# A state-space recurrence taken over pairs of tokens, inside a fused transformer layer

## What is computed

```python
a_bar = jnp.exp(lam * dt)                      # complex, 32 groups x 64 states
b_coef = (a_bar - 1.0) / lam
bu = lax.complex(bu_re, bu_im) * b_coef        # bu_re = einsum('blgi,gni->blgn', u, b_re)
_, state = lax.associative_scan(combine, (a_seq, bu), axis=1)   # s[t] = a_bar s[t-1] + bu[t]
y = einsum(real(state), c_re) - einsum(imag(state), c_im) + d_skip * uf
y = jax.nn.gelu(y); out = y * jax.nn.sigmoid(y @ w_glu + b_glu)
```

## Time and profile before

| | us |
|---|---|
| median of 3 runs | 2065.24 |
| lowest, highest | 2062.25, 2070.86 |
| the profiled execution | 2072.4 |
| its span, first to last instruction | 2070.5 |
| mean granted TensorE clock in it | 0.963 |

### The profile page before, as it was taken

One profiled execution on the slowest core, in us unless ns is written; L12 is line 12 of the kernel. 1 busy time (PEld: TensorE's weight loads), 2 busy tenths in 40 slices (PEclk: granted clock), 3 DMA queues, 4 the chain that ended last, 5 costly groups with the idle time before them and its releaser, 6 DMA issues.

```text
span 2070.5 us, 21878 instructions
## 1 busy us (share of the span) xinstructions
PE 1975.8 (95%) x8614; PEld 1516.5 (73%) x8614; DVE 1247.4 (60%) x1646; ACT 846.2 (41%) x1269; POOL 387.3 (19%) x343
## 2 busy tenths in 40 slices
PE   7999999989977899999999999999999899999997
PEld 5888888766532478888888777776788778766786
DVE  6764344597796445655664776925773468536742
ACT  5331333201445633322333446645552357455531
POOL 2000000156244010100001202512400013214102
PEclk9999999998778899999999989999999999999998
DMA  4232232221000124554552222222122222220221
GB/s 185 85 126 82 95 107 97 85 64 71 26 0 1 66 79 164 196 202 148 198 200 75 82 91 80 82 82 82 52 91 92 97 83 82 91 83 31 92 92 61
DMA packets 53317, 196.69 MB, mean 95 GB/s; under 512 B 5984, under 2 KB 6496, under 8 KB 52704
## 3 DMA queue, kind: packets, MB, share of 16 engines
q1 hardware_dynamic: 43200, 160.55, 22.3%
q0 software_dynamic: 7504, 28.58, 4.1%
q10 hardware_dynamic: 2512, 6.18, 0.9%
HBM read 192.14 MB, written 2.10 MB: 94 GB/s over the span
## 4 chain that ended last, share of the span: by engine, by line
PE 77%; DVE 16%; ACT 4%; issue 2%; POOL 1%; DMA 1%; SPq 0%; POOLq 0%; DVEq 0%; ACTq 0%
PE PS L571 76%; DVE AR L1590 3%; DVE WLO L1587 3%; DVE AR L1823 2%; DVE AR L2072 1%; ACT WHI L1116 1%; PE PS L790 1%; DVE TMP L2146 1%; DVE AR L1913 1%; DVE AR L2039 0%; DVE HNL L1590 0%; DVE ACC L1590 0%; DMA RAW<-in_w13a 0%; DVE H L1975 0%; POOL ACC L2322 0%
## 5 line engine op out<-in xcount | busy, mean ns | idle before, releaser
L1587 DVE TENSOR_TENSOR WLO<-RAW,WHI 128x1024 fp32r<-128x1024 f32 (+1 forms) x272 | 378.3, 1394 | 509.2 <-ACT WHI L1116 509.2
L571 PE MATMUL PS<-HNH,WHI 128*128 128x512 f32 x1632 | 657.9, 403 | 16.0 <-ACT HNH L1147 14.1
L571 PE MATMUL PS<-HNH,WLO 128*128 128x512 f32 x1632 | 640.6, 393 | 3.8 <-DVE WLO L1587 3.8
L1116 ACT ACTIVATE WHI<-RAW 128x1024 fp32r<-128x1024 f32 (+1 forms) x272 | 297.6, 1095 | 648.0 <-PE PS L571 577.1
L571 PE MATMUL PS<-HNL,WHI 128*128 128x512 f32 x1632 | 436.7, 390 | 0.4
L571 PEld LDWEIGHTS PS<-HNH,WHI 128*128 128x128 f32 x1632 | 308.6, 189 | 96.9 <-issue 22.3
L571 PEld LDWEIGHTS PS<-HNH,WLO 128*128 128x128 f32 x1632 | 308.8, 189 | 78.7 <-issue 9.3
L571 PEld LDWEIGHTS PS<-HNL,WHI 128*128 128x128 f32 x1632 | 307.3, 188 | 66.4 <-DVE HNL L1590 2.6
L2202 POOL TENSOR_TENSOR ACC<-ACC,SQ 128x512 f32<-128x512 f32 x46 | 62.9, 1367 | 786.4 <-ACT SQ L1131 785.4
L571 PE MATMUL PS<-AR 128*128 128x512 f32 (+12 forms) x652 | 181.9, 515 | 6.5 <-DVE SQ L1807 5.8
L571 PEld LDWEIGHTS PS<-AR 128*128 128x128 f32 (+5 forms) x652 | 86.3, 203 | 76.8 <-issue 53.0
(11 more groups left out here) (314 smaller groups left out, 2475.6 us busy)
## 6 DMA issues: line engine op xcount, KB each, us to landing
RAW<-in_w_in SPq DMA_DIRECT2D x80, 512.0 KB, 3.5
AR<-in_w_ada POOLq DMA_DIRECT2D x48, 512.0 KB, 3.8
RAW<-in_w13a SPq DMA_DIRECT2D x44, 512.0 KB, 3.2
RAW<-in_w13b SPq DMA_DIRECT2D x44, 512.0 KB, 4.2
RAW<-in_w_out SPq DMA_DIRECT2D x40, 512.0 KB, 3.5
RAW<-in_w2a SPq DMA_DIRECT2D x16, 704.0 KB, 4.1
RAW<-in_w2b SPq DMA_DIRECT2D x16, 704.0 KB, 5.5
RAW<-in_w_inA SPq DMA_DIRECT2D x12, 512.0 KB, 3.3
```

The costliest lines, as they stand in the source:

```text
L571: return pe.matmul(o, l, r, start=start, stop=stop, skip_group_check=True)
L1116: act.activation(hi_of(name, i), raw_of(name, i), ACT.Copy).then_inc(*HI.up(name, i))
L1587: dve.tensor_tensor(lo_of(name, i), raw_of(name, i), f32(hi_of(name, i)), S_).then_inc(*LO.up(name, i))
```

## The change

State is kept at odd tokens only. U is stored with its even tokens first and its odd tokens behind them, 256 each. For a pair (2k, 2k+1) the drive is B u[2k+1] + (a_bar B) u[2k]: two sets of input weights, SA for even and SB for odd tokens, accumulated in PSUM, real and imaginary part side by side in one bank. The scan then runs over 256 pairs with |a_bar| squared, in two chunks of 128; the tables are those of the doubled angle. The output at odd tokens is C' times the state as before. At even tokens it is (C' a_bar) times the state of the pair before, plus a direct product of u[2k] with the 32x32 blocks of C'B (THRU), since the pair's own even state isn't kept. The weights SA, Ca and THRU are computed on the chip: 12 operations of 128x512 more on DVE (three each for CaR, CaI, ATr and ATi), and copies of the results out of PSUM, 8 transposes and 32 products of 32x32 outputs on PE after step 6 of half 0. The schedule of the parameter pieces becomes: two pieces in steps 0 to 3, one in 7 and 8, two in 9 to 12. The output of the mixer is put back in token order when it is split into halves. To make room, OL, U, V_, XAp and the temporaries move; the load of c waits for the last product of w_out.

```diff
 def s5_order():
     for b in range(-1, 9):
         if 0 <= b < 8:
-            for c in range(4):
+            for c in range(2):
                 yield "scan", b, c
...
+            def s5_weights():
+                for z, src in enumerate((ATr, ATi)):
+                    ps, b = take(pe, "s5_a", z)
+                    pe.wait_ge(*V.at("s5_at"))
+                    for y4 in range(4):
+                        t = pe.transpose(ps[:, P * y4:P * y4 + P], src[:, 4 * y4:4 * y4 + 4, :].rearrange("p a b -> p (a b)"), IDENT)
...
+                ps, b = take(pe, "s5_thru")
+                for t16 in range(16):
+                    y4, r = t16 // 4, 32 * (t16 % 4)
+                    o = ps[r:r + 32, P * y4 + r:P * y4 + r + 32]
+                    mm(o, BTr[:, t16, :], CpR[:, t16, :], True, False)
+                    t = mm(o, BTi[:, t16, :], CpI[:, t16, :], False, True)
...
+                        if z == "a" and (half, mi) == (0, 6):
+                            s5_weights()
...
                 elif step == "drive":
                     b, j = at_
-                    mm(psR[:, :], SBr[r, y4, :], U[r, y4, :], True, True).then_inc(*P_.up("drive_re", t16))
-                    psI, bI = take(pe, "drive_im", t16)
-                    mm(psI[:, :], SBi[r, y4, :], U[r, y4, :], True, True).then_inc(*P_.up("drive_im", t16))
...
+                    if j == 0:
+                        bs = [take(pe, "drive", 2 * b + x) for x in range(2)]
+                        for half, (even, odd) in enumerate(((SAr, SBr), (SAi, SBi))):
+                            for e, w in enumerate((even, odd)):
+                                for x, (ps, _) in enumerate(bs):
+                                    r = slice(32 * (2 * (b % 2) + x), 32 * (2 * (b % 2) + x) + 32)
+                                    ts[x] = mm(ps[:, HT * half:HT * half + HT], w[r, y4, :], U[r, y4, HT * e:HT * e + HT], e == 0, e == 1)
...
                 elif step == "read":
+                    mm(ps[r, 0:HT], THRU[r, y4, r], U[r, y4, 0:HT], True, False)
                     for z in range(4):
-                        for j in range(2):
+                        for now in (True, False):
+                            for j in range(2):
...
+                                if now:
+                                    t = mm(o[:, HT:T], w[:, t16, :], x, False, z == 3)
+                                else:
+                                    t = mm(o[:, 1:HT], w[:, t16, :], x[:, 0:HT - 1], False, z == 3)
...
+                tt(RHO, RHO, RHO, M_)
...
+                for o, (x1, y1), (x2, y2), op in ((CaR, (CpR, ar_), (CpI, ai_), A_), (CaI, (CpI, ar_), (CpR, ai_), S_),
+                                                  (ATr, (BTr, ar_), (BTi, ai_), S_), (ATi, (BTi, ar_), (BTr, ai_), A_)):
+                    tt(w1, x1, y1, M_)
+                    tt(w2, x2, y2, M_)
+                    tt(o, w1, w2, op, "s5_at")
+                    if o is CaI:
+                        yield
...
-                    if half == 0 and i < 10:
+                    if half == 0 and (i < 4 or i in (7, 8) or 9 <= i < 13):
                         next(params, None)
-                        next(params, None)
+                        if i not in (7, 8):
+                            next(params, None)
...
                 elif step == "drive":
-                    dve.tensor_tensor(f4(vr), f4(psR[:, :]), c4, M_).then_inc(*V.up("drive_a", t16))
-                    dve.tensor_tensor(f4(t1), f4(psI[:, :]), s4, M_).then_inc(*V.up("drive_b", t16))
-                    dve.tensor_tensor(f4(vi), f4(psI[:, :]), c4, M_).then_inc(*V.up("drive_im", t16))
-                    dve.tensor_tensor(f4(t2), f4(psR[:, :]), s4, M_).then_inc(*V.up("drive", t16))
+                    dve.tensor_tensor(f4(V_[b % 2][:, j, :]), f4(ps[:, :]), c4, M_).then_inc(*V.up("drive_a", t16))
+                    if b:
+                        dve.wait_ge(*G.at("drive_im", t16 - 2))
+                    dve.tensor_tensor(f4(S5T[j]), f4(ps[:, :]), s4, M_).then_inc(*V.up("drive", t16))
...
-                    stt(f4(S5T[k2]), f4(V_[b % 2][1][:, j, :]), -1.0, tables(t16)[1], M_, M_).then_inc(*V.up("back_im", t16))
+                    stt(f2(S5T[j][:, HT:T]), f2(V_[b % 2][:, j, HT:T]), -1.0, tables(t16, 2)[1], M_, M_).then_inc(*V.up("back_im", t16))
...
-            pool.dma_start(AR[:, 4096:6144], D["s5_bc"]).then_inc(*loaded("s5_bc").up())
+            pool.dma_start(AR[:, 4096:5120], D["s5_bc"][:, 0:1024]).then_inc(*loaded("s5_bc").up())
+            pool.dma_start(AR[:, 0:2048], D["s5_bc"][:, 1024:3072]).then_inc(*loaded("s5_bc").up())
+            pool.memset(RR, 0.0).then_inc(*G.up("s5_zero"))
...
                 elif step == "drive":
-                    pool.tensor_tensor(vr, vr, S5T[k1], A_).then_inc(*G.up("drive_re", t16))
-                    pool.tensor_tensor(vi, vi, S5T[k2], S_).then_inc(*G.up("drive_im", t16))
+                    pool.tensor_tensor(vr, vr, S5T[j][:, HT:T], A_).then_inc(*G.up("drive_re", t16))
+                    pool.tensor_tensor(vi, vi, S5T[j][:, 0:HT], S_).then_inc(*G.up("drive_im", t16))
...
-                    pool.tensor_tensor(f4(S5T[2 * j]), f4(vr), s4, M_).then_inc(*G.up("back_re", t16))
-                    pool.tensor_tensor(f4(vr), f4(vr), c4, M_).then_inc(*G.up("back_vr", t16))
-                    pool.tensor_tensor(f4(vi), f4(vi), c4, M_).then_inc(*G.up("back_vi", t16))
+                    pool.tensor_tensor(f2(S5T[j][:, 0:HT]), f2(v[:, 0:HT]), s2, M_).then_inc(*G.up("back_re", t16))
+                    pool.tensor_tensor(f4(v), f4(v), c4, M_).then_inc(*G.up("back_v", t16))
...
+            pool.wait_ge(*P_.at("w_out", KD - 1))
             pool.dma_start(CB, D["c"].partition_broadcast(P)).then_inc(*loaded("c").up())
```

More of the change, by code:

```diff
@@ L468, in sm @@
             return SMALL[:, 16 * i:16 * i + 16]
-        V_ = [[ar(at_v, 2, T) for at_v in pair] for pair in ((9216, 10240), (11264, 12288))]
-        XAp = ar(5120, 2, T)
+        V_ = [ar(10240 + 1024 * i, 2, T) for i in range(2)]
+        XAp = ar(12288, 2, T)
         XBp = ar(19456, 16, 2, 31)
-        CEf = ar(5120, 1024)
+        CEf = ar(12288, 1024)
         CE = CEf.rearrange("p (a b c) -> p a b c", b=8, c=32)
@@ L1614, in s5_params @@
             def s5_params():
-                dt, x, th, k, r, cs, sn, t1, t2, arr, aii, br, bi, den = (sm(i) for i in range(14))
+                dt, x, th, k, r, cs, sn, t1, t2, arr, aii, br, bi, den, are, aim = (sm(i) for i in range(16))
                 lr, li = vec("a_re"), vec("a_im")
@@ L1676, in s5_params @@
                 yield
+                ar_, ai_ = bc(are, 2, b3), bc(aim, 2, b3)
+                for o, (x1, y1), (x2, y2), op in ((CaR, (CpR, ar_), (CpI, ai_), A_), (CaI, (CpI, ar_), (CpR, ai_), S_),
[5 more added lines that the diff above has]
+                        yield
+                tt(t1, cs, cs, M_)
+                tt(t2, sn, sn, M_)
+                tt(sn, cs, sn, M_)
+                tt(cs, t1, t2, S_)
+                ts(sn, sn, 2.0, None, M_)
+                yield
+                for z, o in enumerate((SAr, SAi)):
+                    dve.wait_ge(*P_.at("s5_a", z))
+                    dve.tensor_copy(o, bank("s5_a", z)[:, :].rearrange("p (y n) -> p y n", n=P)).then_inc(*V.up("s5_a", z))
+                yield
+                dve.wait_ge(*P_.at("s5_thru"))
+                dve.wait_ge(*G.at("s5_zero"))
+                for j in range(4):
+                    r = slice(32 * j, 32 * j + 32)
+                    dve.tensor_copy(THRU[r, :, r], bank("s5_thru")[r, :].rearrange("p (y o) -> p y o", o=P)[:, :, r]).then_inc(*V.up("s5_thru", j))
+                yield
+                dve.wait_ge(*G.at("sq", "n1", 7))
+                mine()
                 dve.tensor_copy(TC[:, :, 0:1], cs.unsqueeze(2)).then_inc(*V.up("s5"))
@@ L1814, in dve_program @@
                     b, c = at_
-                    cols = slice(P * c, P * c + P)
                     if c:
```

129 lines of the change are left out of this document (73 added, 56 removed).

## The result

The changed kernel takes 2015.53 us (median of 4 runs, 2012.11 to 2018.64) against 2063.74 for the kernel before (4 runs, 2061.61 to 2070.86): ratio 0.976, 95% interval 0.973 to 0.979, 48 us faster. The forecast was 25 us faster. The direction and the place were right and the size was off by about two: 2015.5 lies outside the forecast's own range (2026 to 2054) and inside the outer one (2012 to 2060). The profiled execution of the changed kernel took 2012.11 us, that of before 2072.4, so the two profiles stand 60 us apart where the medians stand 48: the one is the shortest of its four runs, the other longer than all four of the kernel before.

A forecast was written before the change was run, and what follows sets the result against it. TensorE was taken to bound the kernel, with VectorE causing gaps and half clock in the mixer stage. The stage's -34 us and +9 of overhead made -25 from the 2065.24 us median: 2040 us, range 2026 to 2054.

The forecast's parts named there:

- the outer one: Whole kernel: the wider range of 2012 to 2060 us, leaving out only the more extreme rival outcomes.
- DVE's total: Mixer stage, VectorE: shorter drive, scans, carries and back step save 69 us, so 213 becomes about 144.
- POOL's total: Mixer stage, GpSimd: half of its 107 us of recurrence work, 53 us, goes, leaving it near 72.
- PE's work: Mixer stage, TensorE: full-clock work goes from 186 to 174 us, drives saving 15.7 and the read adding 3.4.
- 2 x 1.98 us: Mixer stage, TensorE: time taken for one pass's drive before the change, expected to become 2.0 us.
- Waits and clock: Mixer stage, TensorE: waits fall from 34 to 21 us, clock rises from 0.82 to 0.85; stage 226 us against 260.
- Rival B: Mixer stage: the clock recovers as gaps fall, 52 us less there, kernel at 2022 us; chance 0.12.
- Rival C: Mixer stage: VectorE's relief thins TensorE's work and lowers the clock, kernel slower, 2097 us at clock 0.70; chance 0.06.
- D: First feed-forward block: its weight split comes late, +24 us before the mixer, kernel at 2055 us; chance 0.09.
- Overhead: Before the mixer: parameter work 2, TensorE's transposes and tiny products 6, start 1, together 9 us more.
- The tail: Attention and output work behind the recurrence, the 74 us after 666 us: no change.
- My own bounds: Mixer stage: wrong if it shrinks under 14 or over 52 us, or clock is under 0.80 or over 0.93.

The follow-up runs named there:

- e10: The kernel before with GpSimd's recurrence adds and multiplies done for only 256 of 512 columns: 2045.82 us, ratio 0.9896.
- e8: The kernel before with VectorE's and GpSimd's recurrence work done for only 256 of 512 columns, TensorE's read kept at full size: 2014.74 us, ratio 0.9746.
- e7: The kernel before without the scans and carries of the last two of each block's four column groups: 2049.59 us, ratio 0.9931.
- e14: The changed kernel with TensorE made to wait, behind the drives of the last four passes, for VectorE's multiplies: 2048.39 us, ratio 0.9906.
- e4: The kernel before with the drive matmuls of a pass's two tiles alternating between their row groups: 2073.81 us, ratio 1.005.
- e2a: The changed kernel with 32 added VectorE multiplies of 128x512, two behind each drive step: 2044.52 us, ratio 0.9907.
- e3: The changed kernel with GpSimd's first multiply of each back step done five times instead of once: 2053.86 us, ratio 0.9954.

## Why the prediction was right or wrong

**DVE's total** was right: 139 us for 144 forecast, from 212.8. The drive fell by 21.8 us for 19.2 (32 instructions, 21.7 us, where 64 took 43.5), the scans by 33.0 for 35.8, the carries by 5.3 for 6, the back step from 17.6 to 9.3, 8.3 for 8. Together these are 68.4 for 69. The other 5.5 us came from instructions that nobody changed and that ran shorter. The eight 248-wide additions took 693 ns after the change, 728 in e10 with only POOL's work halved, and before:

```profile
L1869 DVE TENSOR_TENSOR AR<-AR,VEC 128x248 f32<-128x248 f32 x8 | 7.3, 974 | 0.0
```

The Trainium skill's estimate (VectorE: DVE Perf Modes, the TRN2 errata) of 0.42 us for 256 elements holds for e8's drive multiplies, 417 ns, but not for the back step's 592 ns, another instruction, with two SBUF operands beside POOL's.

**POOL's total** was right, 75.6 for about 72. But what it does was not costed. The forecast gave POOL's relief no price beyond the halved scans; e10 has it at 19 us, more than leaving out half of DVE's scans gave in e7 (14.5).

**PE's work** was wrong: 174 forecast, 187.2 measured. The failing term is "2 x 1.98 us". That row is one tile (x4); PE's timeline has x8 rows of 1.99 us for whole passes, and in six of the eight the tiles stood side by side. The drive gave about 4 us (6 x 1.99 + 2 x 3.96 = 19.9 before, 16 after, at full clock) and not 15.7, and the longer read, costed at 3.4, took it back. The drive after, 2.00 us, was as forecast.

**Waits and clock** were wrong, and this step is the miss: "so I leave 21", "with a third fewer gaps I take 0.85". The forecast held that attention's own chain keeps most of the waits and with them the low clock. In fact the waits fell to 9.4 us and the clock rose to 0.97: 187.2 / 0.97 + 9.4 = 202 us in place of 174 / 0.85 + 21 = 226. With DVE's and POOL's relief alone e8 has 10.4 and 0.95, so most of what was taken for attention's own waits hung on these two engines. Had PE's work been 174, the same error would have shown a gain of 70 us; the two errors stood against each other. Rival B named the right mechanism, with its price of 52 us for a stage that lost 57, and got 0.12. Its "against" was a row of the stretch behind the recurrence at 0.88, which stayed near it (0.91) and had nothing to say about the stretch before. What the forecast lacked is the price of a wait. Over the runs of the table the loss to the clock is 0.6 to 1.3 times the waits, and e14 shows that waits bring loss; here an edit that took 25 us of waits took 35 us of loss with it. But this is no rate for single edits: e7 took 2.6 us of waits and 20 of loss, e4 added 10.6 us of waits and took 3 of loss. What PE runs there matters too: 15 of the 40.6 us of loss before lay in the one stretch from 528 us, with next to no waits, and it is gone. And the forecast was closer than its reasons: with the right work of 187 us its own waits and clock give 187 / 0.85 + 21 = 241 us, 10 us less for the kernel and not 25.

**Rival C** (DVE's relief thins PE's work and lowers the clock) didn't come: the changed kernel is among the lightest on DVE and POOL and has the highest clock. Thin work matters all the same, as the stretches from 466 and 528 us show. **D** didn't come: PE waited 1.81 us behind the 9.51 us block, +2 as costed. **Overhead** was 3.3 and not 9 us: PE's transposes and tiny products took 1.9 us for 6. The row used for their price was at half clock, and 64 records of 32 columns run at 13 ns each beside each other. The start moved nothing that can be told. **The tail** was right, 74.0 us. **My own bounds**: the stage shrank by 57 ("wrong over 52") and its clock is 0.97 ("wrong over 0.93"); both alarms rang.

## What to carry to other kernels

Split a stretch into waits, loss to the clock and full-clock work before pricing an edit: a wait on TensorE is paid more than once (11 us of forced waits cost 16 to 20 us in the stage), work added to TensorE about once (15 us cost 18). Relief of whatever TensorE waits for is worth more than the wait, and how much more depends on the work behind it: look where the half-clock stretches lie, not only at their sum. Price POOL's and VectorE's relief together where their instructions overlap. And look for every row of a pattern before multiplying one of them: x4 and x8 with the same duration were the answer here.

## What the runs showed of the hardware

- The clock can drop behind short waits, and doesn't always. It fell at a wait of 1.30 us, with two shorter ones behind it (e2a), and at one of 2.57 us (e14), for 24 and 10 us; behind another of 2.57 us in e14 it stayed at its high level. The Trainium skill, TensorE: Matmul & The Clock Gate, "HAM oscillation — how this bites in real kernels", describes waits that send TensorE back to its low clock and a penalty on top of the wait; the runs agree that there is such a penalty. Over whole stages the loss was 0.6 to 1.3 times the waits.
- The clock can also drop with no wait before it (466 us of the kernel before, 20 us after the last wait), and a half-clock stretch can be far longer than the waits in it: 31 us in the kernel before with 1.5 us of waits.
- POOL's multiplies slow the vector engine's instructions with two SBUF operands and leave those that read one operand from PSUM alone. From the changed kernel to e3 the 248-wide addition of two SBUF operands went from 693 to 1017 ns and the scans from 661 to 785, the drive multiplies from PSUM from 679 to 684. It works both ways: beside e2a's added vector multiplies POOL's additions went from 817 to 1228 ns. The Trainium skill, SBUF — State Buffer, "Who interferes with whom", says just this: such an instruction contends with a GpSimd instruction that reads SBUF, through a shared read port, and one with at most one SBUF input, outside the two-port modes, doesn't. Here the rows and the page agree, and the forecast would have gained by it: of DVE's 74 us of relief, some 20 are POOL's doing by e10.
- Matmuls on different groups of 32 rows overlap even when issued one tile after the other, up to a point: two of 512 columns per tile overlap fully (1.99 us for two tiles, 1.98 for one), four of 256 per tile take 2.96 us, against 2.00 when alternated.
